# Output projections by token tile, with the next norm, its transposes and the router done per tile, in a two-layer hybrid encoder

## What is computed

```python
def rms_norm(x, g):
    y = x * lax.rsqrt(jnp.mean(x * x, -1, keepdims=True) + RMS_EPS)
    return y * g

x = x + mixer(rms_norm(x, norm_mix[l]))          # mixer ends in "mixed @ w_out", 1024 x 1024
h = rms_norm(x, norm_ffn[l])
group = argmax(softmax(h @ wg1 + bg1))           # 4 groups
fine = (h @ wg2 + bg2)[group]                    # 8 experts in each
top_p, top_e = top_k(softmax(fine), 2)
gate = top_p / sum(top_p) * p_group
x = x + sum over the 2 experts: gate * ((silu(h @ w_gate[e]) * (h @ w_up[e])) @ w_down[e])
```

## Time and profile before

| what | value |
|---|---|
| runs, median (range) | 2171.18 us (2168.29 to 2173.24), 3 runs |
| the profiled execution | 2172.41 us, its span 2170.7 us |
| PE busy | 1893.5 us, 87% of the span |
| DVE, ACT, POOL busy | 726.3, 420.1, 65.8 us |
| granted TensorE clock, mean | 0.925 of full speed |
| DMA | 459.73 MB, 212 GB/s over the span |

### The profile page before, as it was taken

How to read it: one execution, slowest core, us unless ns; L and a number is a source line. 1 busy time by engine, 2 the same in 40 slices (tenths; PEclk the granted TensorE clock), 3 DMA queues, 4 the chain that set the end, 5 groups by cost and what they waited for, 6 DMA issues and landing times.

```text
span 2170.7 us, 23655 instructions
## 1 busy us (share of the span) xinstructions
PE 1893.5 (87%) x9336; PEld 971.7 (45%) x9336; DVE 726.3 (33%) x1230; ACT 420.1 (19%) x844; POOL 65.8 (3%) x104
## 2 busy tenths in 40 slices
PE   6997199999984979999999984977987999999994
PEld 3443188888861453333333332466543333333331
DVE  2137866667625132111111113577114111111112
ACT  3116322222220021111111112234121111111110
POOL 3120000000000000000000001000000000000001
PEclk9997599999985969999999996998887999999997
DMA  8000000000011408999999968210023999999995
GB/s 266 0 0 0 0 1 1 0 0 0 1 54 56 171 30 353 429 429 429 429 428 429 428 280 309 78 39 1 0 78 143 419 430 428 429 428 430 428 428 188
DMA packets 68250, 459.73 MB, mean 212 GB/s; under 512 B 18732, under 2 KB 19878, under 8 KB 43622
## 3 DMA queue, kind: packets, MB, share of 16 engines
q1 hardware_dynamic: 55114, 433.77, 48.3%
q10 hardware_dynamic: 10780, 16.86, 2.1%
q0 software_dynamic: 2304, 8.39, 1.2%
HBM read 440.11 MB, written 18.87 MB: 211 GB/s over the span
## 4 chain that ended last, share of the span: by engine, by line
PE 79%; DVE 11%; ACT 6%; issue 2%; DMA 1%; ACTq 0%; POOL 0%; DVEq 0%; POOLq 0%
PE bank L580 20%; PE bank L598 11%; PE bank L554 10%; PE bank L1616 7%; PE bank L1728 4%; PE bank L784 3%; PE bank L1736 3%; PE bank L1810 3%; PE bank L863 3%; PE bank L562 2%; ACT hT L363 2%; PE bank L1744 1%; PE bank L1759 1%; DVE ring L1554 1%; DMA arena<-expert_rows,dest 1%
## 5 line engine op out<-in xcount | busy, mean ns | idle before, releaser
L580 PE MATMUL bank<-ring,arena 128*64 128x512 f32 x2048 | 450.4, 592 | 1.6 <-DVE arena L438 1.6
L491 DVE TENSOR_TENSOR arena<-arena,bank 64x512 f32<-64x512 f32 x64 | 68.3, 1067 | 648.1 <-ACT arena L371 648.0
L580 PEld LDWEIGHTS bank<-ring,arena 128*64 128x64 f32 x2048 | 146.8, 137 | 293.3 <-issue 291.3
L554 PE MATMUL bank<-xn,arena 128*64 128x512 f32 x1024 | 235.8, 602 | 7.4 <-DVE arena L491 5.0
L598 PE MATMUL bank<-ring,arena 128*64 128x512 f32 x1024 | 239.1, 610 | 0.9 <-ACT arena L375 0.9
L1616 PE MATMUL bank<-hT,ring 128*128 128x512 f32 x336 | 144.5, 592 | 0.8 <-ACT hT L242 0.8
L554 PEld LDWEIGHTS bank<-xn,arena 128*64 128x64 f32 x1024 | 74.2, 139 | 156.7 <-issue 130.1
L598 PEld LDWEIGHTS bank<-ring,arena 128*64 128x64 f32 x1024 | 69.1, 139 | 125.6 <-issue 124.3
L371 ACT ACTIVATE arena<-bank 64x512 f32<-64x512 f32 x64 | 37.8, 590 | 401.1 <-PE bank L580 401.1
L438 DVE TENSOR_TENSOR arena<-bank,gffn 128x512 f32<-128x512 f32 x64 | 44.3, 692 | 189.0 <-PE bank L562 189.0
L1728 PE MATMUL bank<-ring 128*128 128x128 f32 x768 | 101.2, 284 | 5.4 <-DVE ring L1549 4.5
(11 more groups left out here) (308 smaller groups left out, 1948.7 us busy)
## 6 DMA issues: line engine op xcount, KB each, us to landing
ring<-in_moe_w_gate_dram SPq DMA_DIRECT2D x64, 2048.0 KB, 10.7
ring<-in_moe_w_up_dram SPq DMA_DIRECT2D x64, 2048.0 KB, 15.4
ring<-in_moe_w_down_dram SPq DMA_DIRECT2D x64, 2048.0 KB, 12.8
expert_rows<-arena ACTq DMA_DIRECT2D x128, 128.0 KB, 8.0
ring<-in_rec_w_in_dram SPq DMA_DIRECT2D x5, 2048.0 KB, 13.1
ring<-in_att_w_in_dram SPq DMA_DIRECT2D x3, 2048.0 KB, 11.8
ring<-in_rec_w_out_dram SPq DMA_DIRECT2D x2, 2048.0 KB, 10.4
ring<-in_att_w_out_dram SPq DMA_DIRECT2D x2, 2048.0 KB, 18.9
```

The source lines that it names most:

```text
L491: nc.vector.tensor_tensor(hb[0:CAP, par, :].rearrange("s (f p) -> s p f", f=4), sg[0:CAP, par, :].rearrange("s (p f) -> s p f", f=4), bank ...
L554: mm = nc.tensor.matmul(bank[2][h * CAP:(h + 1) * CAP, :], onehot[:, par, t, :], xn[:, t, h * 512:(h + 1) * 512], start=(t == 0), stop=(t ...
L580: mm = nc.tensor.matmul(bank[par][k * CAP:(k + 1) * CAP, :], xg[:, par, c, :], W[k][:, c * FF:(c + 1) * FF], start=(c == 0), stop=(c == KC ...
```

## The change

The output projections run by tile: for each tile both halves. After the first half of tile t, PE transposes the normed tile t-1; after the second half, PE runs the router of tile t-1. The norm is cut up by tile: ACT squares a tile and takes its root, DVE scales it into a new buffer `xm`, PE transposes its 8 chunks into banks 0 and 1, and the gain copy is split: DVE takes chunks 0 to 3 in one instruction (`dve_hT`), ACT chunks 4 to 7 in four of 128 columns (`act_hT`). The combining of experts runs by tile too (k inside t), with norm 2 of the finished tiles between the adds. The buffer `xn` now holds the gathered rows, `xm` the normed tokens. The tables of the router (`dve_tables`, and PE's product that spreads the biases) move ahead of the output projection of layer 0. The last output tiles are stored as they finish. The diff, cut (the removed functions stand above; the projection of layer 1 is changed as the last piece shows for layer 0):

```diff
         def act_norm(act, j):
             for t in range(TT):
+                if j == 0:
+                    act.wait_ge(x_loaded[t // 2], 16)
+                else:
+                    act.wait_ge(x_updated, 8 * (j - 1) + 2 * t + 2)
+                act_norm_tile(act, j, t)
+
+        def act_norm_tile(act, j, t):
+            nc.scalar.activation(XN[j][:, t, :], X[:, t, :], ACT.Square, accum_out=ssq[:, t:t + 1]).then_inc(ssq_ready, 1)
+            act.wait_ge(ssq_ready, TT * j + t + 1)
+            nc.scalar.activation(rstd[:, t:t + 1], ssq[:, t:t + 1], ACT.Sqrt, scale=1.0 / D, bias=eps_rms).then_inc(rms_ready, 1)
+
+        def dve_norm(dve, step, j, t):
+            dve.wait_ge(rms_ready, TT * j + t + 1)
+            step(nc.vector.reciprocal(rstd[:, t:t + 1], rstd[:, t:t + 1]))
+            src, dst = X[:, t, :], XN[j][:, t, :]
+            if j % 2:
+                src = src.rearrange("p (q c) -> p c q", c=KC)
+                dst = dst.rearrange("p (c q) -> p c q", c=KC)
+            nc.vector.tensor_scalar(dst, src, rstd[:, t:t + 1], None, ALU.mult).then_inc(xn_ready, 1)
+
+        def pe_turn_norm(pe, j, t):
+            pe.wait_ge(xn_ready, TT * j + t + 1)
+            if t:
+                pe.wait_ge(hT_ready, KC * j + 2 * t)
+            for c in range(KC):
+                mm = nc.tensor.transpose(bank[c // 4][:, (c % 4) * P:(c % 4 + 1) * P], XN[j][:, t, c * P:(c + 1) * P], ident[:, :])
+                if c % 4 == 3:
+                    mm.then_inc(hT_raw, 1)
+
+        def dve_out_norm(dve, step, j, done):
             for t in range(TT):
+                for h in range(2):
+                    i = 2 * t + h
+                    dve.wait_ge(done, i + 1)
+                    x = X[:, t, h * 512:(h + 1) * 512]
+                    nc.vector.tensor_tensor(x, x, bank[4 + i % 4][:, :], ALU.add).then_inc(x_updated, 1)
+                    if t and not h:
+                        dve_hT(dve, j, t - 1)
+                dve_norm(dve, step, j, t)
+            dve_hT(dve, j, TT - 1)
+
+        def act_out_norm(act, j):
+            for t in range(TT):
+                act.wait_ge(x_updated, 8 * (j - 1) + 2 * t + 2)
+                act_norm_tile(act, j, t)
+                if t:
+                    act_hT(act, j, t - 1)
+            act_hT(act, j, TT - 1)
+
+        def act_hT(act, j, t):
             if j == 1:
                 act.wait_ge(gffn_loaded, 32)
+            act.wait_ge(hT_raw, KC * j + 2 * t + 2)
+            for c in range(4, KC):
+                ins = nc.scalar.activation(hT[:, c, t * P:(t + 1) * P], bank[1][:, (c - 4) * P:(c - 3) * P], ACT.Copy,
+                                           scale=GAIN[j][:, c:c + 1])
+            ins.then_inc(hT_ready, 1)
+
+        def dve_hT(dve, j, t):
+            if j == 1:
+                dve.wait_ge(gffn_loaded, 32)
+            dve.wait_ge(hT_raw, KC * j + 2 * t + 1)
+            nc.vector.tensor_tensor(hT[:, 0:4, t * P:(t + 1) * P], bank[0][:, :].rearrange("p (c t) -> p c t", c=4),
+                                    GAIN[j][:, 0:4].unsqueeze(2).to_broadcast([P, 4, P]), ALU.mult).then_inc(hT_ready, 1)
...
-        rows, at = carve(AR, at, [4, D])
+        xm, at = carve(AR, at, [TT, D])
+        rows = xn
...
 
-            for k in range(2):
-                for t in range(TT):
-                    i = k * TT + t
+            for t in range(TT):
+                for k in range(2):
+                    i = 2 * t + k
                     dve.wait_ge(rows_loaded[i % 4], 16 * (2 * l + i // 4 + 1))
                     nc.vector.scalar_tensor_tensor(X[:, t, :], rows[:, i % 4, :], wtok[:, k, t:t + 1], X[:, t, :],
                                                    ALU.mult, ALU.add).then_inc(x_updated, 1)
                     dve.wait_ge(x_updated, 8 + 16 * l + i + 1)
+                if l == 0 and t:
+                    dve_norm(dve, step, 2, t - 1)
+                if l == 0 and t >= 2:
+                    dve_hT(dve, 2, t - 2)
+            if l == 0:
+                dve_norm(dve, step, 2, TT - 1)
+                dve_hT(dve, 2, TT - 2)
+                dve_hT(dve, 2, TT - 1)
 
         def pool_moe(pool, l):
             pool.wait_ge(route_ready, l + 1)
             for par in range(2):
                 pool.wait_ge(ob_stored[par], 32 * NPAIR * (l + 1))
             pool.wait_ge(over_end, l + 1)
...
                     if i >= 4:
                         pool.wait_ge(x_updated, 8 + 16 * l + i - 3)
                     nc.gpsimd.indirect_dma_start(rows[:, i % 4, :], None, expert_rows[l][:, :],
-                                                 bass.IndirectOffsetOnAxis(ap=dest[:, i:i + 1], axis=0)
+                                                 bass.IndirectOffsetOnAxis(ap=dest[:, n:n + 1], axis=0)
                                                  ).then_inc(rows_loaded[i % 4], 16)
+
+        def pe_router(pe, l, t):
+            pe.wait_ge(hT_ready, KC * (1 + 2 * l) + 2 * t + 2)
+            if l == 0 and t == 0:
+                pe.wait_ge(router_loaded, 160)
+            for c in range(KC):
+                mm = nc.tensor.matmul(bank[2][:, t * 36:(t + 1) * 36], hT[:, c, t * P:(t + 1) * P], wr[:, l, c, :],
+                                      start=(c == 0), stop=(c == KC - 1))
...
+                mm.then_inc(lg_done, 1)
 
         def pe_moe(pe, l):
             m = moe[l]
-            pe_turn_norm(pe, 1 + 2 * l)
-            pe.wait_ge(hT_ready, KC * (2 + 2 * l))
-            if l == 0:
-                pe.wait_ge(router_loaded, 160)
-            for t in range(TT):
...
-        FIRST = ([[(gn_out, FT)], [], [], [], [(out_done, 4)], [(out_done, 8)]],
+        FIRST = ([[(gn_out, FT)], [], [], [], [(out_done, 8)], [(out_done, 8)]],
                  [[(m0["down_done"], EXPERTS)], [(att_proj, 4)], [(att_proj, 8)], [(att_proj, 14)],
-                  [(att_out_done, 4)], [(att_out_done, 8)]])
+                  [(att_out_done, 8)], [(att_out_done, 8)]])
...
-                sp.wait_ge(x_updated, 29 + t)
+                sp.wait_ge(x_updated, 26 + 2 * t)
                 y = (y_prompt, y_sample)[t // 2]
...
+            for t in range(TT):
+                act_hT(act, 0, t)
 
...
-            dve_norm(dve, step, 0)
+            for t in range(TT):
+                dve_norm(dve, step, 0, t)
+                if t:
+                    dve_hT(dve, 0, t - 1)
+            dve_hT(dve, 0, TT - 1)
...
+            dve_tables(dve, step)
+            dve_out_norm(dve, step, 1, out_done)
             dve_rest(dve, step)
 
...
-            for h in range(2):
-                pe.wait_ge(slot_loaded[h], 32)
-                W = slot[h].rearrange("p (c f) -> p c f", c=KC)
-                for t in range(TT):
-                    i = h * TT + t
+            pe.wait_ge(brow_loaded, 80)
+            nc.tensor.matmul(bank[3][:, 0:HEADS + 72], ones[0:1, :], brow[0:1, :], start=True, stop=True).then_inc(bb_raw, 1)
+            for t in range(TT):
+                for h in range(2):
+                    i = 2 * t + h
+                    if t == 0:
+                        pe.wait_ge(slot_loaded[h], 32)
+                    W = slot[h].rearrange("p (c f) -> p c f", c=KC)
                     if i >= 4:
                         pe.wait_ge(x_updated, i - 3)
                     for c in range(KC):
                         mm = nc.tensor.matmul(bank[4 + i % 4][:, :], mixT[:, c, t * P:(t + 1) * P], W[:, c, :],
                                               start=(c == 0), stop=(c == KC - 1))
                     mm.then_inc(out_done, 1)
+                    if t:
+                        (pe_router(pe, 0, t - 1) if h else pe_turn_norm(pe, 1, t - 1))
+            pe_turn_norm(pe, 1, TT - 1)
+            pe_router(pe, 0, TT - 1)
             pe_rest(pe)
```

More of the change, by code:

```diff
@@ L159, in row @@
             return v.rearrange("(n p) -> n p", p=P)
-        x_loaded, vec_loaded, brow_loaded, rgw_loaded, rgw_zero, router_loaded = (
-            sem(n) for n in ("x_loaded", "vec_loaded", "brow_loaded", "rgw_loaded", "rgw_zero", "router_loaded"))
+        vec_loaded, brow_loaded, rgw_loaded, rgw_zero, router_loaded = (
+            sem(n) for n in ("vec_loaded", "brow_loaded", "rgw_loaded", "rgw_zero", "router_loaded"))
+        x_loaded = [sem(f"x_loaded{s}") for s in range(2)]
         slot_loaded = [sem(f"slot{i}_loaded") for i in range(SLOTS)]
@@ L238, in act_hT @@
+        def act_out_norm(act, j):
[6 more added lines that the diff above has]
+        def act_hT(act, j, t):
             if j == 1:
                 act.wait_ge(gffn_loaded, 32)
-            for c in range(KC):
-                act.wait_ge(hT_raw, KC * j + c + 1)
-                nc.scalar.activation(hT[:, c, :], bank[c % 2][:, :], ACT.Copy,
-                                     scale=GAIN[j][:, c:c + 1]).then_inc(hT_ready, 1)
+            act.wait_ge(hT_raw, KC * j + 2 * t + 2)
[3 more added lines that the diff above has]
+            ins.then_inc(hT_ready, 1)
@@ L515, in pool_moe @@
             pool.wait_ge(over_end, l + 1)
```

(20 more changed lines are left out.)

82 lines of the change are left out of this document (21 added, 61 removed).

## The result

The changed kernel takes 2175.39 us (median of 20 runs, 2170.24 to 2179.31), the kernel before beside it 2171.11 (20 runs, 2164.56 to 2174.0): ratio over all runs 1.0018, 95% interval 1.001 to 1.0025. That is 4.3 us slower by the medians (0.20%): small, but the interval leaves out 1. The forecast was 2176.6. The profiled execution has a span of 2174.4 us, 3.7 more than before.

The account below looks back on a forecast made before the run. PE, 79% of the span, was taken as the bound, so its idle seams count. Terms +3.3, +4.3, -5.5, +3.3 and 0 gave +5.4 on 2172.41, 2177.8; the median, 1.2 lower, was forecast at 2176.6 us, range 2162 to 2186.

Parts of the forecast that it names:

- the three chances: Whole kernel against the one before: faster 0.22, within 0.27, slower 0.51; slower begins at 2175.5, faster ends at 2166.8.
- The waits of PE at the router: Output projections: PE waits three times each for ACT's copy, 3.5 us a wait, bounds 3.3 and 3.8.
- The clock: Output projections: clock lost at each gap, router lots cold at 3.2 us, two cold groups costing 4.2 per projection.
- The seams: Output projection to router logits: layer 0 90.7 us against 87.4, +3.3; layer 1 90.0 against 85.7, +4.3.
- Combining: Layer 0's expert combining to attention's first product: 7.6 us earlier, first projections cold +2.1, in all -5.5.
- cold start: A group of products beginning at the lower clock, priced at 2.1 us, also behind the first norm and the combining.
- The first norm: Start to first projection: 27.9 plus hand-over 0.1 against 26.78, +1.2; first group cold +2.1; in all +3.3.
- The rule of the Trainium skill: Projections behind norms 0 and 2 would have started cold before too; two cold starts drop out, -4.2; set aside.
- The clock did not hold: Rival at the seams: the clock holds in the gaps, -16.6, 2154.6 us; chance 0.12.
- nor come back at once: Rival: clock falls but returns within the router or at once in the group, routers 2.7; -5.8, 2165.4 us; chance 0.15.
- The end did not get worse: Rival: stores and last gathers collide, +3, first experts start at a worse clock, +2; 2181.6 us; chance 0.10.
- What the change means to do: Rival: router lots find copies ready; layer 0 71.0 us, layer 1 70.3, in all -34.0, 2137.2 us; chance 0.02.

Follow-up runs that it names:

- Experiment 1: The changed kernel, but ScalarE copies tile t-1 before it squares tile t in both output projections; 2147.72 us, ratio to before 0.9883.
- experiment 2: The changed kernel with four extra 512-column products that nobody reads filling PE's wait before each router of tiles 0 to 2; 2156.77 us, ratio 0.9924.
- experiment 4: The changed kernel with layer 0's combining and the norm behind it done as before; 2182.13 us, ratio 1.0048.
- experiment 5: The changed kernel with two pairs of banks for the transposes of the first norm and the norm behind the combining; 2163.84 us, ratio 0.9969.
- experiment 3: The changed kernel with the first norm alone done as before; 2173.16 us, ratio to the kernel before 1.0004.
- experiment 7: The changed kernel with gathers, adds and stores of layer 1 alone as before; 2175.2 us.

## Why the prediction was right

The time (2176.6 against 2175.39) and the range held, and it came out of the mechanism that the text named. That it came within 1.2 us is partly luck: terms of the sum were off by up to 1 us in both directions. The likeliest of the three chances, slower by over 0.2%, just missed (slower began at 2175.5), as the sum was 1.8 us too high in the profiles (+5.4 against the table's +3.6).

- **The waits of PE at the router.** Forecast three of 3.5 us per projection, measured 3.31 to 3.32; the parts too (add to square 0.73, square 1.2, root 0.3, four copies 1.12). Experiment 1 removed their cause and with it 14 to 16 us a seam.
- **The clock.** Forecast: lost at each gap, routers at 3.2, two cold groups at 2.1 each. Measured in layer 0: routers of 2.90, 2.39, 3.46 and 3.63, groups longer by 9.57 - 7.03 = 2.5 and 8.40 - 7.03 = 1.4; in layer 1 by 2.1 and 2.7. So the mean of the routers is 3.1 in layer 0 and 3.0 in layer 1, of the groups 2.2. The reason that I gave was partly wrong: I read from the earlier trace rows that 36-column products don't hold the clock. In experiments 1 and 2 they do, for lots of 16 rows, when no gap stands ahead of them. The gap pulls it down; the router is where it arrives.
- **The seams.** +2.3 and +3.3 where the sum said +3.3 and +4.3. Too large were the waits, by 0.2 us each, six of them, and the routers of layer 0 by 0.4, of layer 1 by 0.8.
- **Combining.** From last add to first product 16.2 became 8.2, the last add came 0.4 later: -7.6, as forecast, and +2.2 for the cold start. The sum takes the cold start as lost; in the five profiles named in experiment 4 only 0.4 of it was left at attention's end. (The other 1.1 of the table's -8.7 lies in the dispatch and the experts of layer 0, which were not touched.) The serial order of transposes and copies in one pair of banks was as forecast, and experiment 5 shows what it cost there, 8.17 - 5.95 = 2.2 us.
- **The first norm.** The start at 27.99 was forecast (28.0), by parts that made up for each other: ACT's last root ended at 17.1 and not 17.5, a copy took 1.1 and not 1.2, and ACT waited 2.1 us for each lot of transposes and not 1.9. The cold start was mis-sized: 3.0 instead of 2.1, since here 7 rows ran at the lower level, the 2.1 came from a projection that had the clock back sooner. It also varies: six other profiles with this norm had 146.5 to 147.5 us for the 336 rows.
- **The rule of the Trainium skill** that I had weighed and set aside ("TensorE: Matmul & The Clock Gate", Part 4: transposes don't count as busy for the gate): by it the projection behind the first norm starts cold whatever is done there. Experiments 3 and 5 start it hot, 336 rows in 144.48 us. For these float32 transposes the trace disagrees with the rule, which that page of the Trainium skill gives with a time for bf16.
- **The rivals.** The clock did not hold, nor come back at once (router means of 3.0 and 3.1, not 2.7). The end did not get worse (experiment 7). What the change means to do, priced at 71.0 us for layer 0, takes 73.4 once ACT's order is turned round: the price was right within 2.4 us, the order in the change kept it from showing.
- **Not forecast:** stages that the change doesn't touch moved by +1.4, -1.1, -1.8 (attention behind its cold start) and -0.1, -1.6 in all; most of the sum's 1.8 lies there, the rest in terms that were off both ways: -1.0 for each seam, +0.9 for the first norm's cold start, +0.8 at the end.

## What to carry to other kernels

When work is cut up by tile and woven into another engine's stream, look at the queue of each helper engine: a short instruction for the tile before, put behind one that waits for the tile now, hands that wait to whoever needs it. Here one swap of two calls made a change that costs 0.2% into one that gains 1.2%, and with a second pair of banks 1.7%. Where PE has to wait, half of the price may be the clock behind the gap; a filled gap tells the two apart.

## What the runs showed of the hardware

- Clock and gap: with a gap of 3.3 us the clock fell to its lower level (0.51 in the window shown) within the router lot behind it and was full again some 4 us later, in another place some 7; with the same 3.3 us filled by 512-column products, or with no gap, it stayed at 1.00 through 16 rows of 36 columns.
- Transposes alone raised it: 0.20 to 0.11 us per load in experiment 5; four lots with 1.7 to 1.9 us without a load between them did not.
- The PEclk column says 1.00 for the first 34 us of the changed kernel, while the first 7 rows took 6.29 us, 0.90 each, where at full clock a row takes 0.43. At the start of a span the duration of a row tells the clock, not the column. The rows:

```profile
28.00:30.00 2.00, 2.00 (x3) 0.97 (x4) 0.00 (x0) 1.95 (x4) 0.00 (x0) 1.00 1.06 390
30.00:32.00 2.00, 2.00 (x4) 0.88 (x3) 0.69 (x4) 1.17 (x2) 0.00 (x0) 1.00 1.05 387
```

- Stages that no edit touched moved between executions of one kernel: attention 211.5 and 207.2, 212.4 and 207.2, 202.7 and 205.4 us. Part of such a difference can also come back with the kernel, as the clock of 0.73 did in both profiles of experiment 1. A gain of a few us is read at its seam, and in the total only over many runs.
